# The first layer's gate as row sums on VectorE, in place of four blocks on TensorE

## What is computed

```python
def ada_mod(cond, w, b):
    m = jax.nn.silu(cond) @ w + b
    return jnp.split(m[..., None, :], 3, axis=-1)

    for i in range(DEPTH):
        shift, scale, gate = ada_mod(c, ada_w[i], ada_b[i])
        c_shift, c_scale, c_gate = ada_mod(c_ctx, ada_w[i], ada_b[i])
        h = rms_norm(x, norm_w[i]) * (1.0 + scale) + shift
        hc = rms_norm(ctx, norm_w[i]) * (1.0 + c_scale) + c_shift
        ...
        x = x + gate * o
        if need_ctx_out:
            ctx = ctx + c_gate * oc
```

## Time and profile before

| | |
|---|---|
| median of 3 runs | 2425.8 us (2420.58 to 2426.4) |
| the profiled execution, its time | 2424.95 us |
| its span, first to last instruction | 2423.1 us |
| TensorE busy in the span | 2336.0 us (96%) |
| VectorE, ScalarE, GpSimd busy | 45%, 47%, 48% |
| mean granted TensorE clock | 0.987 of full speed |
| DMA engines' mean share | 41% of the span for the kernel's queue |

### The profile page before, as it was taken

One profiled execution on the slowest core, in us unless ns is written; L12 is line 12 of the kernel. 1 busy time (PEld: TensorE's weight loads), 2 busy tenths in 40 slices (PEclk: granted clock), 3 DMA queues, 4 the chain that ended last, 5 costly groups with the idle time before them and its releaser, 6 DMA issues.

```text
span 2423.1 us, 59202 instructions
## 1 busy us (share of the span) xinstructions
PE 2336.0 (96%) x25854; PEld 1941.8 (80%) x25854; DVE 1097.6 (45%) x2337; ACT 1128.7 (47%) x2042; POOL 1162.7 (48%) x634
## 2 busy tenths in 40 slices
PE   6999999999999978999999999999999999999997
PEld 2576777777778856788888888888888888888997
DVE  3143344333340037555555655555555555553223
ACT  3343333333342237654565456644664466544443
POOL 2232333333335545456644765466546664563544
PEclk9999999999999989999999999999999999999998
DMA  9855555555543221233323332333223322336553
GB/s 375 322 210 208 196 209 215 189 184 189 205 188 125 87 96 49 104 109 105 109 84 106 106 114 72 107 106 114 93 94 105 115 98 82 114 106 235 191 183 115
DMA packets 99347, 352.15 MB, mean 145 GB/s; under 512 B 10768, under 2 KB 15248, under 8 KB 96784
## 3 DMA queue, kind: packets, MB, share of 16 engines
q1 hardware_dynamic: 99088, 348.36, 40.8%
HBM read 336.13 MB, written 12.19 MB: 144 GB/s over the span
## 4 chain that ended last, share of the span: by engine, by line
PE 90%; DVE 4%; DMA 2%; ACT 2%; issue 1%; POOL 1%; SPq 0%; DVEq 0%; ACTq 0%
PE bank L884 9%; PE bank L886 8%; PE bank L885 8%; PE bank L695 8%; PE bank L697 8%; PE bank L696 8%; PE bank L981 4%; PE bank L652 3%; PE bank L1124 2%; PE bank L924 2%; PE bank L925 2%; PE bank L926 2%; PE bank L1126 2%; PE bank L1125 2%; PE bank L1093 2%; PE bank L1078 2%
## 5 line engine op out<-in xcount | busy, mean ns | idle before, releaser
L479 POOL TENSOR_TENSOR wl<-raw,wh 128x1024 fp32r<-128x1024 f32 x215 | 517.2, 2413 | 615.3 <-ACT wh L474 615.3
L884 PE MATMUL bank<-hh,wh 128*128 128x512 f32 (+1 forms) x1040 | 409.8, 394 | 19.5 <-DVE hl L1834 14.4
L407 POOL TENSOR_TENSOR wl<-raw,wh 128x1024 fp32r<-128x1024 f32 x85 | 207.3, 2448 | 405.3 <-ACT wh L402 405.1
L886 PE MATMUL bank<-hh,wl 128*128 128x512 f32 (+1 forms) x1040 | 381.5, 367 | 1.6 <-issue 1.5
L885 PE MATMUL bank<-hl,wh 128*128 128x512 f32 (+1 forms) x1040 | 380.8, 366 | 0.0
L474 ACT ACTIVATE wh<-raw 128x1024 fp32r<-128x1024 f32 x232 | 245.6, 1061 | 277.4 <-PE bank L926 121.4
L695 PE MATMUL bank<-hh,wh 128*128 128x512 f32 x864 | 345.7, 400 | 5.9 <-ACT scratch L1511 3.3
L697 PE MATMUL bank<-hh,wl 128*128 128x512 f32 x864 | 337.6, 391 | 0.0
L696 PE MATMUL bank<-hl,wh 128*128 128x512 f32 x864 | 337.3, 390 | 0.0
L884 PEld LDWEIGHTS bank<-hh,wh 128*128 128x128 f32 x1040 | 197.5, 190 | 60.3 <-issue 15.1
L886 PEld LDWEIGHTS bank<-hh,wl 128*128 128x128 f32 x1040 | 197.3, 190 | 35.7 <-issue 1.9
(11 more groups left out here) (299 smaller groups left out, 4531.1 us busy)
## 6 DMA issues: line engine op xcount, KB each, us to landing
raw<-w_in SPq DMA_DIRECT2D x259, 512.0 KB, 3.6
raw<-w_ada SPq DMA_DIRECT2D x101, 512.0 KB, 5.4
raw<-w_out SPq DMA_DIRECT2D x84, 512.0 KB, 3.6
scratch<-w_ada SPq DMA_DIRECT2D x59, 512.0 KB, 5.9
scratch<-keep_g SPq DMA_DIRECT2D x15, 1024.0 KB, 5.7
scratch<-w_in SPq DMA_DIRECT2D x23, 512.0 KB, 6.9
raw<-w_gate SPq DMA_DIRECT2D x22, 512.0 KB, 5.2
scratch<-xT SPq DMA_DIRECT2D x2, 4096.0 KB, 12.9
```

Source lines behind the costliest of these rows:

```text
L407: eng.tensor_tensor(fl[h % SPLIT], ring[ring_slot("half", h)], fh[h % SPLIT].bitcast(F32), ALU.subtract)\
L479: eng.tensor_tensor(buffers(s)[1], raw[:, s % RAW, :], buffers(s)[0].bitcast(F32), ALU.subtract)\
L884: pe.matmul(ps, w[:, k * P:(k + 1) * P], hhv[:, kk, t0:t1], start=first and k == k0, stop=False)
L886: done = pe.matmul(ps, r[:, k * P:(k + 1) * P], hhv[:, kk, t0:t1], start=False, stop=last and k == k1 - 1)
```

## The change

Layer 0's gate (blocks 8 to 11) leaves the late blocks, which are eight now, two times four eighths in a group instead of three. In its place `w_gate` holds the turned gate columns of both layers: 64 units instead of 32. A unit of layer 1 is used as before, by two sums; a unit of layer 0 by four, since both conditions need it, and between the two sums on one piece VectorE waits for the first (`ch.link`), whose products go to the scratch tile `a_mod`. `mrow` is loaded and passed through silu for both conditions.

```diff
-LATE = [8, 9, 10, 11] + list(range(MODBLK, 2 * MODBLK - 4))
+LATE = list(range(MODBLK, 2 * MODBLK - 4))
...
-UNITS = 2 * KT
+UNITS = 4 * KT
+UNITAT = [0, 4, 7, 8, 8, 8]
...
-    for u in range(2, 4):
+    for u in range(2, 8):
         unit(u)
-    eighths(len(EARLY), 8, 12)
     for g in range(1, GROUPS):
         h0, e0 = 4 * KVH + 10 * g, 8 * len(EARLY) + PERGROUP * g
         for t in range(5):
             half(h0 + 2 * t)
             half(h0 + 2 * t + 1)
-            if t < 2:
-                for u in range(4 * g + 2 * t, 4 * g + 2 * t + 2):
-                    unit(u)
-            if 1 <= t < 4:
+            for u in range(8 * g + UNITAT[t], 8 * g + UNITAT[t + 1]):
+                unit(u)
+            if 1 <= t < 3:
                 eighths(0, e0 + 4 * (t - 1), e0 + 4 * t)
...
                 if n:
                     late_ada(PERGROUP * n + 4, PERGROUP * n + 8)
                     front_tile(h + 6, pb[1][:, :])
-                    late_ada(PERGROUP * n + 8, PERGROUP * n + 12)
...
-                else:
-                    late_ada(8, 12)
...
-                j, pair = u // (KT // 2), u % (KT // 2)
+                j, layer, pair = u // KT, 1 - u % 8 // 4, u % KT // 8 * 4 + u % 4
...
-                    done = dve.tensor_tensor_reduce(unit[:, vs], unit[:, vs], mrow[1], 1.0, acc if j else bias,
-                                                    ALU.mult, ALU.add, acc)
+                    for s in range(layer, 2):
+                        acc = mod[:, tile, s:s + 1]
+                        done = dve.tensor_tensor_reduce(unit[:, vs] if s else a_mod, unit[:, vs], mrow[s], 1.0,
+                                                        acc if j else bias, ALU.mult, ALU.add, acc)
+                        if s == 0:
+                            ch.link(done)
...
-                gate_rows(g)
+                for u in range(2 * g, 2 * g + 2):
+                    gate_rows(u)
...
             for n in range(GROUPS):
                 if n:
-                    gate_rows(4 * n)
-                    gate_rows(4 * n + 1)
+                    for u in range(8 * n, 8 * n + 4):
+                        gate_rows(u)
                     b_merge(n - 1)
-                    gate_rows(4 * n + 2)
-                    gate_rows(4 * n + 3)
+                    for u in range(8 * n + 4, 8 * n + 7):
+                        gate_rows(u)
...
                    .then_inc(sem("v_var"), 1)
+                dve.wait_ge(sem("v_var"), n + 1)
+                for u in range(8 * n + 7, 8 * n + 8) if n else range(4, 8):
+                    gate_rows(u)
                 dve.wait_ge(sem("v_root"), n + 1)
...
-                if n == 0:
-                    gate_rows(2)
-                    gate_rows(3)
```

More of the change, by code:

```diff
@@ L234, in build @@
         a_ug = cut(T)
-        a_vsq = a_ug
+        a_vsq = a_mod = a_ug
         a_ga = cut(T)
@@ L518, in crow_load, with unit_loads @@
                 if j:
[L519 to L523, removed]
+                    sp.wait_ge(sem("unit_done"), KT * j)
+                for s in range(2):
+                    sp.dma_start(mrow[s], cond_row[s:s + 1, j * T:(j + 1) * T].to_broadcast([P, T])).then_inc(sem("x_in"), 16)
+            def unit_loads(first, end):
+                for v in range(first, end):
                     ring_load(sp, "unit", v, w_gate[v, :, :])
             crow_load(0)
-            unit_loads(0)
+            unit_loads(0, 2)
             late_loads(4, 8)
             half_loads(w_in0, 0, PIECES0 + 4, PIECES0 + 6)
-            unit_loads(2)
-            late_loads(8, 12)
+            unit_loads(2, 8)
             for n in range(1, GROUPS):
                 h = HMIX + 10 * n
[L534 to L539, removed]
+                for t in range(5):
                     if t == 4 and n % 2 and n < GROUPS - 1:
@@ L542, in _ @@
                     half_loads(w_in0, 0, h + 2 * t, h + 2 * t + 2)
+                    unit_loads(8 * n + UNITAT[t], 8 * n + UNITAT[t + 1])
+                    if 1 <= t < 3:
+                        late_loads(PERGROUP * n + 4 * (t - 1), PERGROUP * n + 4 * t)
             half_loads(w_out0, HOUT, HOUT, HOUT + 4)
@@ L1855, in gate_rows @@
             def gate_rows(u):
-                j, pair = u // (KT // 2), u % (KT // 2)
+                j, layer, pair = u // KT, 1 - u % 8 // 4, u % KT // 8 * 4 + u % 4
                 unit = ring[ring_slot("unit", u)]
                 ring_wait(dve, "unit", u)
-                dve.wait_ge(sem("crow_ready"), j + 1)
+                dve.wait_ge(sem("crow_ready"), 2 * j + 2)
                 if j:
-                    dve.wait_ge(sem("unit_done"), u - KT // 2 + 1)
+                    dve.wait_ge(sem("unit_done"), u - KT + 1)
                 for v in range(2):
-                    tile = GATE + 2 * pair + v
-                    acc = mod[:, tile, 1:2]
+                    tile = (3 * layer + 2) * KT + 2 * pair + v
                     bias = sm[:, SO["ada_b"][0] + tile:SO["ada_b"][0] + tile + 1]
                     vs = slice(v * T, (v + 1) * T)
-                    done = dve.tensor_tensor_reduce(unit[:, vs], unit[:, vs], mrow[1], 1.0, acc if j else bias,
-                                                    ALU.mult, ALU.add, acc)
+                    for s in range(layer, 2):
[4 more added lines that the diff above has]
+                            ch.link(done)
                 done.then_inc(sem("unit_done"), 1)
@@ L2573 @@
     h1 = np.concatenate(stream, 0)
-    gate = np.asarray(ada_w[1])[:, 2 * D:].T.reshape(KT // 2, 2, P, 4, T).transpose(3, 0, 2, 1, 4).reshape(UNITS, P, 2 * T)
+    gate = [np.asarray(ada_w[l])[:, 2 * D:].T.reshape(2, 4, 2, P, 4, T).transpose(4, 0, 1, 3, 2, 5) for l in (1, 0)]
+    gate = np.stack(gate, 2).reshape(UNITS, P, 2 * T)
     arrays = {
         "xT": xT, "w_ada": np.stack([eighths(np.asarray(ada_w[l])) for l in range(2)]), "w_in0": h0, "w_gate": gate,
-        "cond_row": np.asarray(c[0]).reshape(1, D),
+        "cond_row": np.stack([np.asarray(c_ctx), np.asarray(c[0])]),
         "w_out0": halves(np.asarray(ab_w_out[0])), "w_in1": h1, "w_out1": halves(np.asarray(dn_w_out[0])),
```

6 lines of the change are left out of this document (4 added, 2 removed).

## The result

| | before | after |
|---|---|---|
| median, same chip | 2425.7 us | 2498.5 us (2492.7 to 2500.29) |
| ratio of after to before | | 1.0296 [1.028, 1.0312] |
| the profiled execution, its span | 2423.1 us | 2497.1 us |
| opening stage, up to the first matmul of k | 156.26 | 159.81 |
| from there to the first `attend` | 64.86 | 80.77 |

The change costs 2.96%; 2.9% was forecast. The span grew by 74.0 us: 6 x 7.81 = 46.9 in groups 1 to 6, 8.5 in group 7, 15.9 in group 0, 3.55 in the opening stage, and 0.8 less behind the groups.

The account below looks back on a forecast made before the run. TensorE, busy 96% of the span, was taken to bound the kernel. Groups 1 to 7 at 7 x 7.85 = +55 us and group 0 at +14.5, added to 2424.95, gave 2495 us, slower by 2.9%; range 2468 to 2526.

Parts of the forecast that it names:

- Half h+7: Tile 4, groups 1 to 7: its load waits for unit 8n+7, so TensorE pauses 7.5 us per group (7.0 to 9.0).
- The clock: Behind each tile 4 pause, groups 1 to 7: half clock costs 2.0 us more per group (1.6 to 2.9; 0 if held).
- The removed lot: Groups 1 to 7: one lot of four late eighths leaves TensorE's path, saving 1.85 us per group.
- The units behind the merge, and half h+4: Groups 1 to 7: three units hide ahead of q's norm; h+4 loads later, costing 0.2 us per group (0 to 1).
- Group 0: Group 0: VectorE waits for units 2 and 3, rotation +10.8 us; +14.5 us in all (11 to 20), removed lot at nothing.
- the gain arrives: Rival: h+7 loads in time, TensorE never stops within tile 4; 2412 us, or 2426 with group 0's wait; chance 0.04.
- The cheaper case: Rival: the waits come, but the clock holds in the pauses and group 0 costs 11; 2472 us, chance 0.12.
- The dearer case: Rival: h+7 wait 9.0, h+4 1.0, clock 2.9, group 0 20; 2522 us, 0.16; with a second wait 2546, 0.05.
- no slowdown: Whole kernel: chance 0.04 as a rival; in the closing sum 0.03 for faster and 0.02 for within 7 us of no change.

Follow-up runs that it names:

- e_sum: The kernel after, with unit 8n+7 summed ahead of the norm of q in groups 1 to 7, ring order kept; 2430.0 us, 1.002 of before.
- e_chain: The kernel after, with unit 8n+7 given two sums instead of four from group 2 on (part of the gate missing); 2479.5 us, 1.0225 of before.
- e_gain: The kernel before, without layer 0's gate blocks and nothing in their place (gate set to 0.5); 2416.6 us, 0.9963 of before.
- e_refit: e_sum with group 0 laid out anew: ring order, places of VectorE's sums, late lot in the pause behind the mixing; 2415.5 us, 0.9961 of before.
- e_refit2: e_refit, with ScalarE's next two splits in group 0 held until VectorE has scaled the probabilities; 2417.1 us, 0.9961 of before.
- e_fill: The kernel after, with the second lot of late eighths between tile 4's halves in groups 1 to 7; 2495.5 us, 1.0288 of before.
- e_place2: The kernel after, with unit 8n+7 behind h+7 in the ring and condition row loads behind h+8 and h+9; 2431.0 us, 1.0021 of before.

## Why the prediction was right, step by step

**Half h+7**: right, and the step that decides. Forecast 7.5 us of pause (7.0 to 9.0), measured 7.00, from 6.63 to 7.37. Its links came nearly as costed: the sums 3.0 us (350.58 to 353.60), the load 3.7 (353.63 to 357.37, 3.43 was taken), the split 2.36; from the variance to TensorE's restart 10.4 where 10.0 was said. What came otherwise is the chain's start. I named v's turning; in after the variance starts later than that, behind the rotary embedding on VectorE (347.48, the turning's last record ends at 346.55). And I took the variance's end from a group of before in which one step of that embedding lasted 1.34 us (319.32) beside GpSimd's splits, so that the variance ended 3.1 us behind the start of tile 4; in after it is 2.2 to 3.0. e_sum shows that it is this unit's place, and e_chain that the pause follows the chain's length.

**The clock**: right in kind, too small in size. Forecast 2.0 (0 to 2.9); 2.98 in group 2, 2.7 on the mean (9.67 for the whole wait, by e_sum, less the 7.00 of the pause; the seven second halves of tile 4 give the same mean, from 1.7 in group 4 to 3.1 in group 3). I chose nearer the lower end of 1.6 to 2.9; behind a pause of 7 us the clock is low for 3.4 us and then, in most groups, only partly back. Pause and clock together: 9.5 forecast, 9.7 measured.

**The removed lot**: 1.85 forecast, 2.07 measured in e_gain. The length of the lot's own rows left out what the scores pay for standing behind it.

**The units behind the merge, and half h+4**: 0.2 forecast. The three units took 8.9 us (321.45 to 330.33), 3.0 each. e_sum's group is 0.21 us longer than e_gain's, which does none of layer 0's sums: that is all the rest of VectorE's new work in a group. So a group's sum is 7.00 + 2.67 + 0.21 - 2.07 = 7.81, where 7.85 was forecast; that it meets so closely is in part luck, since the pause came out smaller and the clock and the lot larger than said. The rule of the Trainium skill that I set against it (page SBUF — State Buffer, section "Who interferes with whom": VectorE instructions with two inputs in SBUF and GpSimd's reads exclude each other) would have cost 17 us there, and none of it came, since GpSimd stood idle in that stretch, as argued. Two sums in each group do run beside splits and take 2.9 us (for group 2 at 302.41 and 307.25); they stand ahead of the merge at 320.84, where VectorE has the time. In group 0 the trace agrees with the rule: a sum took 2.83 us beside a split at 204.13, and a product 2.49 in e_gain. The scalings have one large input; the same section counts their operation among those that can take the shared ports too, and e_refit against e_refit2 agrees, 5.37 us beside the splits and 1.41 without.

**Group 0**: +14.5 forecast (11 to 20), +15.9 measured. Counted from the first matmul of k, the rotation came 9.9 later, where 10.8 was said (the terms given add up to 10.6): unit 2 was issued and landed as forecast (3.58 us from 186.60), but unit 3 cost nothing, where I had given it 2 us. The tile came 10.4 later, the turning 14.1 (13 was said), the attend 15.9. One step behind that sum was wrong: I cost the removal of group 0's lot at nothing, because TensorE waits 1.19 us behind it. e_gain shows +4.3 us for it: the lot was cover in a pause, and its four loads spaced the ring so that GpSimd's split missed the merge, as the two traces read; no run takes the two apart. How much of the 4.3 lies in after's 15.9 the runs don't tell, because the collisions fall elsewhere there.

**What the sum left out**: the opening stage ended 3.55 us later in after. Its code is the same; in the kernels run here it ended at 156.1 to 160.1, in no order that follows the edits. The traces show a part of the cause. In the four profiled executions in which it ended at 158.97 or later (after, e_sum, e_fill, e_refit2) the mean granted clock from 76 to 85 us was 0.62 to 0.81, behind a wait of 1.3 to 2.7 us for an eighth's load; in the other eight, which ended by 157.46, it was 1.00 there, and no such wait was longer than 1.6. Why the load comes later in some executions isn't settled. So a difference of 3 to 4 us between two single profiles need not be the edit's.

**The rivals**: "the gain arrives" named 2412 to 2426 and the point from which it decides, the 7.5 us by which the chain would have to be shorter. That is what e_sum, e_place2 and e_refit did by moving the unit, and they gave 2430, 2431 and 2415. The cheaper case failed by its own condition: the clock did not hold, and group 0 cost 15.9 instead of 11. The dearer case, with a second wait in a group, didn't come. The chances have a slip: no slowdown has 0.04 as a rival and 0.03 + 0.02 in the last sum.

So the change has the gain that it seems to have, 1.9 us in each of seven groups. It loses it five times over by where one unit in eight is summed, and a second time by group 0, where there was no room for the work that was moved in.

## What to carry to other kernels

Work moved from a busy engine to an idle one also moves the release of the buffers that it reads. Ask of every moved piece: when is it done now, which load waits for its buffer, what else stands behind that load in the queue, and is what the piece itself waits for earlier or later than that load's consumer? Here an engine half idle made TensorE stop, because its work was queued behind a result that TensorE makes just ahead of asking for the load.

Price a pause at more than its length: in these groups 7.0 us of waiting cost 9.7, and 5.2 cost 7.2. And removing instructions that stand in a pause can cost time, if they space the loads behind them or keep TensorE busy.

## What was not expected of the hardware

- Behind a pause of 7.0 us the loss by the clock was 2.7 us on the mean, behind one of 5.2 us 2.0. In group 2 of both the granted clock was 0.50 for the first 3.4 us; in after it was 0.76 over the next 5.1 us, in e_chain 0.93 over the next 5.3:

```profile
355.30:358.70 3.40, 3.39 (x8) 0.50 0.98 388
358.70:364.00 5.30, 5.30 (x22) 0.93 0.68 214
```

(windows of TensorE in e_chain, group 2). The length of the pause alone doesn't decide it: in after's group 4, behind 6.79 us, the clock was 0.54 for the first 3.4 us and 1.00 over the next 5.1. Why it came back earlier there and in e_chain isn't shown.
- Behind the pause of 1.19 us ahead of e_refit2's turning the granted clock stayed at 1.00; behind the next one, of 2.07 us, it was 0.51 (windows of TensorE in e_refit2):

```profile
210.40:214.10 3.70, 1.53 (x13) 1.00 1.03 417
214.10:217.50 3.40, 3.40 (x8) 0.51 0.77 267
```
